# Prompt attention of a decoder step: branch A's probabilities turned by matrix products with a scaled identity

## The reference, cut to what matters

```python
s = jnp.where(valid, einsum(q, k), -inf)
p = softmax(s)                      # branch A
o_a = einsum(p, v)

p = softmax(scores)                 # branch B
a = p[:, :, 0] - lam * p[:, :, 1]
o_b = rmsnorm(einsum(a, v), subln_g) * (1 - lam_init)
```

## Time and profile before

| | us |
|---|---|
| median of 3 runs | 3218.79 |
| lowest and highest run | 3216.23 and 3221.10 |
| the profiled execution: time, and its span from first to last instruction | 3220.68, 3219.1 |
| TensorE busy in the span | 2871.2 |
| VectorE busy in the span | 1445.2 |
| ScalarE busy in the span | 587.4 |

### The profile page before, as it was taken

One profiled execution on the slowest core, in us unless ns is written; L12 is line 12 of the kernel. 1 busy time (PEld: TensorE's weight loads), 2 busy tenths in 40 slices (PEclk: granted clock), 3 DMA queues, 4 the chain that ended last, 5 costly groups with the idle time before them and its releaser, 6 DMA issues. The chain is left out here.

```text
span 3219.1 us, 69051 instructions
## 1 busy us (share of the span) xinstructions
PE 2871.2 (89%) x26593; PEld 2016.6 (63%) x26593; DVE 1445.2 (45%) x2844; ACT 587.4 (18%) x1308; POOL 678.1 (21%) x1192
## 2 busy tenths in 40 slices
PE   8998979999888669999988799999798799998698
PEld 4764534665566446666755566766566576675698
DVE  2337858995778364333343543333433632002211
ACT  2431112101666010101010110100100201001101
POOL 0131003001200001133432433333333333430000
PEclk9999989999999889999998999999899799999799
DMA  7575239422500857788997989889888796762585
GB/s 230 145 221 189 79 104 304 144 80 68 181 11 17 245 175 248 251 304 294 324 304 268 319 274 310 290 306 309 283 295 277 259 305 229 227 204 90 183 265 193
DMA packets 419890, 708.71 MB, mean 220 GB/s; under 512 B 67985, under 2 KB 230193, under 8 KB 419442
## 3 DMA queue, kind: packets, MB, share of 16 engines
q1 hardware_dynamic: 330674, 470.65, 44.8%
q0 software_dynamic: 75456, 232.86, 21.9%
q10 hardware_dynamic: 13440, 0.85, 0.3%
HBM read 660.01 MB, written 92.13 MB: 234 GB/s over the span
## 5 line engine op out<-in xcount | busy, mean ns | idle before, releaser
L1457 PE MATMUL sa_t<-tw_z,tw_w 128*128 128x304 f32 x2496 | 681.3, 429 | 15.5 <-DVE tw_z L1534 11.1
L1457 PEld LDWEIGHTS sa_t<-tw_z,tw_w 128*128 128x128 f32 x2496 | 471.9, 193 | 196.1 <-issue 44.7
L1735 POOL DMA_DIRECT2D sa_ring_v<-cache_b_kv x512 | 275.2, 537 | 1207.7 <-PE sa_o L1864 813.0
L1457 PE MATMUL sa_t<-tw_x,tw_w 128*128 128x304 f32 x1440 | 405.8, 439 | 41.6 <-DMA tw_w<-packed 35.3
L1975 DVE STREAM_TRANSPOSE sa_key_b<-sa_ring_k 128x2048 f32<-128x2048 f32 x128 | 294.8, 2306 | 260.6 <-PE sa_s L1797 192.5
L1457 PEld LDWEIGHTS sa_t<-tw_x,tw_w 128*128 128x128 f32 x1440 | 278.3, 198 | 149.1 <-issue 62.6
L414 PE MATMUL pr_acc<-pr_w,pr_u_t 128*128 128x512 f32 (+1 forms) x720 | 288.3, 549 | 3.7 <-DVE pr_row L574 3.7
L1736 POOL DMA_DIRECT2D sa_ring_va<-cache_a_kv x512 | 274.1, 535 | 54.1 <-issue 27.4
L874 PE MATMUL sel_g<-sel_u,sel_gw 128*128 128x352 f32 x768 | 227.5, 460 | 0.0
L1797 PE MATMUL sa_s<-sa_key_b,sa_q_pad 32*32 32x256 f32 x8192 | 189.2, 410 | 26.2 <-DVE sa_key_b L1975 19.5
L874 PEld LDWEIGHTS sel_g<-sel_u,sel_gw 128*128 128x128 f32 x768 | 146.1, 190 | 81.7 <-issue 0.8
(11 more groups left out here) (334 smaller groups left out, 3475.7 us busy)
## 6 DMA issues: line engine op xcount, KB each, us to landing
sa_ring_k<-cache_b_kv SPq DMA_DIRECT2D x512, 256.0 KB, 3.9
sa_ring_v<-cache_b_kv POOLq DMA_DIRECT2D x512, 256.0 KB, 6.3
tw_w<-packed SPq DMA_DIRECT2D x228, 512.0 KB, 6.6
tp_w<-packed SPq DMA_DIRECT2D x76, 512.0 KB, 4.3
sa_ring_ka<-cache_a_kv SPq DMA_DIRECT2D x512, 64.0 KB
sa_ring_va<-cache_a_kv POOLq DMA_DIRECT2D x512, 64.0 KB, 6.1
packed<-w_gate_up POOLq DMA_DIRECT2D x44, 512.0 KB, 14.3
tw_w<-packed SPq DMA_DIRECT2D x48, 256.0 KB, 7.3
```

Source lines behind the costliest of these rows:

```text
L1457: ins = pe.matmul(bank[:, 0:self.width], self.w[:, at % self.SLOTS, k - lo, :], moving[:, k, :], start=(k == 0), stop=(k == depth - 1))
L1735: pool.dma_start(ring_v[:, n % RING, :], rows_of(cache_b, page, 1)).then_inc(v_in[n // 4 % 2], 16)
```

## The change

Branch A's probabilities are divided while they are turned. VectorE's mix of an A unit makes two identities with their rows multiplied by the inverse sums (spread), and TensorE turns a block by a plain product with spread in place of a transposition with ident. The product with line 1090 goes, and out only copies. In VectorE's step out now comes before mix and is of unit s - 4 in place of s - 3; the loops of all engines have one step more, and the stores and ROOT are one step later. ScalarE's fifth and later units wait for scaled or mixed in place of o_read.

```diff
-    ROOT = 8 * LAST + 3
+    ROOT = 8 * LAST + 4
...
-        inverse_of = ph.sb("inverse_of", [P, 2, 2, DH])
+        inverse_a = ph.sb("inverse_a", [P, 2])
+        spread = ph.sb("spread", [P, 2, 2, P])
...
                 def transposes(u):
                     if kind == "a":
-                        pe.wait_ge(exped, 2 * u + 2)
+                        pe.wait_ge(scaled, u // 2 + 1)
...
-                            ins = pe.transpose(t_bank[n % 2][:, b - lo, :], src[:, b * P:(b + 1) * P], ident[:])
+                            if kind == "a":
+                                ins = pe.matmul(t_bank[n % 2][:, b - lo, :], src[:, b * P:(b + 1) * P], spread[:, u // 2 % 2, m], start=True, stop=True)
+                            else:
+                                ins = pe.transpose(t_bank[n % 2][:, b - lo, :], src[:, b * P:(b + 1) * P], ident[:])
...
                 def values(u):
-                    if kind == "a":
-                        pe.wait_ge(scaled, u // 2 + 1)
-                        pe.matmul(scale_a, inverse_of[:, u // 2 % 2]..., ident[:], start=True, stop=True, skip_group_check=True)
...
-                                ins = pe.matmul(o_a[rows], va[:, b, rows], prob_t[...], start=False, stop=(b == i),
+                                ins = pe.matmul(o_a[rows], va[:, b, rows], prob_t[...], start=(b == 0), stop=(b == i),
...
                 def exps(u, m):
                     if u >= 4 and m == 0:
-                        act.wait_ge(o_read, u - 3)
+                        act.wait_ge(*((scaled, u // 2 - 1) if UNITS[u][1] == "a" else (mixed, b_before[u - 4] + 1)))
...
                 def mix(u):
                     if kind == "a":
                         dve.wait_ge(exped, 2 * u + 2)
+                        nc.vector.reciprocal(inverse_a[:], total[:, u % 4, :])
+                        dve.drain()
                         if u >= 4:
-                            dve.wait_ge(pv_done, u - 3)
-                        nc.vector.reciprocal(inverse_of[:, u // 2 % 2], total[:, u % 4, :]...to_broadcast([P, 2, DH])).then_inc(scaled, 1)
+                            dve.wait_ge(turned, turned_by[u - 4])
+                        for m in range(2):
+                            ins = nc.vector.tensor_scalar(spread[:, u // 2 % 2, m], ident[:], inverse_a[:, m:m + 1], None, ALU.mult)
+                        ins.then_inc(scaled, 1)
...
                 def out(u):
-                        nc.vector.tensor_copy(scale[:], scale_a)
-                        dve.drain()
-                        nc.vector.tensor_tensor(o_ta[:, k % 2, r, :], o_a, scale[:], ALU.mult).then_inc(o_read, 1)
+                        nc.vector.tensor_copy(o_ta[:, k % 2, r, :], o_a).then_inc(o_read, 1)
...
-                for s in range(U + 3):
+                for s in range(U + 4):
                     if s < U:
                         mask(s)
+                    if s >= 4:
+                        out(s - 4)
                     if 1 <= s < U + 1:
                         mix(s - 1)
-                    if s >= 3:
-                        out(s - 3)
```

More of the change, by code:

```diff
@@ L1024, in prompt_attend @@
         weight = ph.sb("weight", [P, 2])
-        inverse_of = ph.sb("inverse_of", [P, 2, 2, DH])
+        inverse_a = ph.sb("inverse_a", [P, 2])
+        spread = ph.sb("spread", [P, 2, 2, P])
         squares = ph.sb("squares", [P, P])
-        scale = ph.sb("scale", [P, P])
         ms = ph.sb("ms", [P, TILES * H_B])
@@ L1035, in prompt_attend @@
         o_bank = [ph.ps(f"o{c}", [P, 512]) for c in range(2)]
-        o_a, scale_a, o_b = o_bank[0][:, 0:P], o_bank[0][:, P:2 * P], o_bank[1][:, 0:P]
+        o_a, o_b = o_bank[0][:, 0:P], o_bank[1][:, 0:P]
         packed = ph.sem("packed")
@@ L1087, in values @@
                         pe.wait_ge(o_read, u - 1)
-                    if kind == "a":
-                        pe.wait_ge(scaled, u // 2 + 1)
-                        pe.matmul(scale_a, inverse_of[:, u // 2 % 2].rearrange("p m d -> p (m d)"), ident[:], start=True, stop=True, skip_group_check=True)
                     pe.wait_ge(t_copied, turned_by[u])
@@ L1095, in values @@
                                 rows = slice(m * DH, (m + 1) * DH)
-                                ins = pe.matmul(o_a[rows], va[:, b, rows], prob_t[:, u % 2, m, b, :], start=False, stop=(b == i),
+                                ins = pe.matmul(o_a[rows], va[:, b, rows], prob_t[:, u % 2, m, b, :], start=(b == 0), stop=(b == i),
                                                 tile_position=(0, m * DH), skip_group_check=True)
@@ L1114, in _ @@
                         transposes(s - 2)
-                    if s >= 3:
+                    if 3 <= s < U + 3:
                         values(s - 3)
@@ L1154, in copy_tile @@
                     act.sem_inc(b_copied, 1)
-                for s in range(1, U + 3):
+                for s in range(1, U + 4):
                     if s - 1 < U:
@@ L1190, in store_b @@
                     sp.dma_start(a["o_t"][512:1024, i * P:(i + 1) * P].rearrange("(h e) t -> e h t", e=P), o_tb[:, j % 2]).then_inc(b_stored[j % 2], 16)
-                for s in range(U + 3):
-                    if s >= 9 and (s - 9) % 8 == 0 and (s - 9) // 8 < TILES:
-                        store_a((s - 9) // 8)
+                for s in range(U + 4):
+                    if s >= 10 and (s - 10) % 8 == 0 and (s - 10) // 8 < TILES:
+                        store_a((s - 10) // 8)
                     if 0 <= s - ROOT - 1 < LAST:
@@ L1219, in mix @@
                         dve.wait_ge(exped, 2 * u + 2)
+                        nc.vector.reciprocal(inverse_a[:], total[:, u % 4, :])
+                        dve.drain()
                         if u >= 4:
-                            dve.wait_ge(pv_done, u - 3)
-                        nc.vector.reciprocal(inverse_of[:, u // 2 % 2], total[:, u % 4, :].rearrange("p (m o) -> p m o", o=1).to_broadcast([P, 2, DH])).then_inc(scaled, 1)
+                            dve.wait_ge(turned, turned_by[u - 4])
+                        for m in range(2):
+                            ins = nc.vector.tensor_scalar(spread[:, u // 2 % 2, m], ident[:], inverse_a[:, m:m + 1], None, ALU.mult)
+                        ins.then_inc(scaled, 1)
                         return
```

## The result

| | before | after |
|---|---|---|
| median of 4 runs each, us | 3217.75 | 3250.89 |
| lowest and highest | 3216.23, 3221.10 | 3247.73, 3255.82 |
| the profiled execution: time, span | 3220.68, 3219.1 | 3247.73, 3246.1 |

The ratio is 1.0103 (95%: 1.0085 to 1.012): the change costs 33 us by the medians, 27 by the two profiled executions. The forecast was 3246, its range 3230 to 3264.

A forecast was written before the change was run, and what follows sets the result against it. No single engine was taken to bound the stage: a VectorE-TensorE chain in small-A pairs, TensorE in large ones. Periods gave +25.8 us, one clock fall brought +27.5, added to the median 3218.79: 3246, own range 3236 to 3256, with rivals 3230 to 3264.

The forecast's parts named there:

- Price of a product: A's turned blocks on TensorE: 0.235 us a product, +0.118 a block over a transposition, +34.0 us for 288 blocks.
- doubt about four times: A's turned blocks: by the skill's fourfold transposing speed a product would take 0.47 us, adding 101 us in place of 34.
- The new wait: A's products wait for VectorE's scaled identity: 1.60 us from the end of B's masks, TensorE's wait near 1.0 in A0.
- Periods: Eight tile-pair periods in the prompt's attention: sum 66.23 us against 59.77, +6.46.
- From periods to stage: Eight periods, each four times, make up the attention stage: +6.46 becomes +25.8 us.
- The clock: TensorE's granted clock in the stage: one more fall after idling, 1.7 us.
- The end of the stage: Stage ends and later stores: same instructions, costed at nothing; uncovered, one store's wait would be about 1 us.
- One to one into the span: Attention stage, closed by barriers on both sides: its gain or loss goes fully into the span, nothing else touched.
- Only large A tiles pay: Rival, 12 in 100: scaling ready in time, small pairs unchanged, four large ones grow; +12.7 us, 3231.5.
- Clock falls in A0 to A2: Rival, 13 in 100: each of these 12 pairs loses 1.5 us at half clock; +18 more, 3263.
- VectorE's relief decides: Rival, 2 in 100: products cost no more than transpositions, 0.60 us a pair saved 32 times; 3199.6.
- Fourfold: Rival, 1 in 100: a product takes four transpositions' time on TensorE; +91 us, about 3310.

The follow-up runs named there:

- e1: Kernel before, with A's blocks turned by plain products with the unscaled identity, division and line 1090 kept; 3283.64 us, ratio 1.0179.
- e3: Changed kernel with VectorE's order put back to mask, mix, out (out still of unit s - 4); 3247.41 us, ratio 1.0078 to before.
- e2: Changed kernel with A's blocks turned by plain transpositions, still waiting for the scaled identity, A's output undivided; 3250.78 us, ratio 1.0086 to before.
- f1: e1 with 48 small unread products (192 TensorE instructions) added at the stage's end; ratio 1.0072 to before, median 21.4 us above it.
- g4: e4 with 128x2 reciprocal, ScalarE's earlier wait, and output after mix in steps masking A's tiles 5 to 7; ratio 0.9999 to before.
- f3: Changed kernel with 16 small unread products (64 TensorE instructions) added at the stage's end; ratio 1.0079 to before, median 26.3 us above it.
- e4: Kernel before with only the order changed: out of unit s - 4 ahead of mix, steps and stores one later; 3220.51 us, ratio 1.0001.
- g2: e3 with 16 small unread products (64 TensorE instructions) added at the stage's end; ratio 1.0081 to before, median 22.5 us above it.
- f2: Kernel before with 16 small unread products (64 TensorE instructions) added at the stage's end; ratio 1.0126, median 41.2 us above before.
- g1: e2 with 32 small unread products (128 TensorE instructions) added at the stage's end, A's output undivided; ratio 1.0003 to before.

## Why the prediction was right, and where it was off

- **Price of a product: right.** Sixteen products go from 847.49 to 851.26, 0.236 each, for 0.235 taken. e1's stage, with products and nothing else, grew by 24.4. The second pass of each f32 product is the change's whole cost in the stage. The forecast's doubt about four times (the Trainium skill, TensorE: Matmul & The Clock Gate, section Terms) is answered by these rows: twice.
- **The new wait: right in kind, near in size.** From the end of the B masks to the products it is 1.47 for 1.60, the wait 0.84 for 1.0. Of it, at A0, B's output ahead of the scaling costs 0.70: the difference between the third and the fourth period of A0 after (7.65, when no B output exists yet, and 8.36) and between after and e3 (7.66). e2 shows that outside A0 and A1 wait, order and the loss of line 1090 together are level or a gain, up to 0.27 a pair.
- **Periods: the sum right (66.42 for 66.23), single ones off by up to 0.47.** A7 is 0.16 longer, because the lone B transposition takes 0.26 up to the next start (852.00 to 852.26) and not 0.12. A4 was taken for a chain of VectorE's (8.15) and is TensorE's, 8.05 of 8.62 busy. A2 and A3 are 0.25 and 0.34 shorter: the branch over ScalarE was drawn too long. These cancel.
- **From periods to stage: too high.** 25.8 became 22.3. The first two periods of the stage, while the pipeline fills and the clock is not yet full, took 8.01 and 8.00 us, 8.00 and 7.97 before, and the third has no B output yet (7.65 for 7.41), so the four pairs of A0 grew by 1.2 and not by 4.0. That was the pipeline's filling, which "eight periods, each four times" passes over.
- **The clock: its price right, its sign wrong.** One more fall was expected, +1.7. Instead two of before went. Busy times of before and of after around them (A7's and the last tile's stretches):

```profile
825.19:859.64 34.45, 30.76 (x254) 22.26 (x254) 23.38 (x69) 21.57 (x53) 14.91 (x18) 0.95 0.77 241
...
1010.25:1036.96 26.71, 22.91 (x176) 16.74 (x176) 21.27 (x62) 18.64 (x42) 0.00 (x0) 0.94 0.09 21
```

```profile
826.98:862.75 35.77, 33.70 (x296) 26.32 (x296) 21.68 (x75) 22.00 (x50) 14.52 (x18) 1.00 0.75 232
...
1029.47:1055.67 26.20, 23.74 (x195) 17.50 (x193) 17.80 (x60) 18.05 (x42) 0.00 (x0) 1.00 0.06 11
```

  In the first, four pairs of A7 cost 1.3 instead of 4 x 0.76 = 3.0; in the second three pairs of A4 became 0.5 shorter. The waits that had stood ahead of the falls were 1.66 and 2.24 at 1029.58. The first is 1.49 in after, and that the shorter wait saved the clock is not shown. e1 and f1 run the same instructions up to there, and the same wait of 1.67 has a fall behind it in e1 and none in f1; the eight transposes show it:

```profile
829.96 1.82 PE L1084 MATMUL att_t<-keep_ident,att_diff 128*128 128x128 f32 x8 [1.67 <-DVE att_diff L1236]
```

```profile
830.73 1.09 PE L1084 MATMUL att_t<-keep_ident,att_diff 128*128 128x128 f32 x8 [1.67 <-DVE att_diff L1238]
```

  The granted clock in the 2 us from there was 0.55 and 1.00, and the two periods around it took 20.31 and 18.74: one fall costs 1.6 us, and whether it comes behind this wait differs between two executions of the same stage. g4 had one behind 1.30, and f3, the changed kernel's own stage, had one in A1 (a period of 9.05 for 8.10). The second fall went with its wait. The wait is gone in e4, where only the order differs (that period is 8.53 for 11.66), and it is 1.63 without a fall in e1, where only the products differ (10.63). So the order alone takes that wait away, and the first fall was lost by luck.
- **The end of the stage: costed at nothing, 4.1 longer in this execution.** From A4's last scores on it takes 30.4 instead of 26.2. Of that 1.4 comes with the products alone (27.6 in e1) and was counted in the four times eight periods. The rest is the doubt of the forecast, "uncovered, one store's wait would be about 1 us": it was uncovered. All of B's tiles are turned a step later, so the last ones come close on each other, and ScalarE waits for the store of a tile two earlier; ScalarE and TensorE after:

```profile
1077.61 0.58 ACT L1151 COPY att_o_tb<-att_t 128x512 f32<-128x512 f32 x1 [2.26 <-DMA o_t<-att_o_tb]
1078.66 0.20 ACT L1175 ACTIVATE att_root<-att_ms 128x4 f32<-128x4 f32 x1 [0.46 <-issue]
```

```profile
1080.34 1.11 PE L1107 MATMUL att_t<-keep_ident,att_o_rows 128*128 128x128 f32 x4 [5.77 <-DVE att_o_rows L1267]
```

  The root behind that copy is late, so TensorE's last wait is 5.77 where it was 3.02 at 1057.51. Most of that belongs to this one execution: the same store's wait is 0.42 in f3, e3 and g2, where TensorE's last wait is 3.7 to 3.9 and the end takes 28.5 to 28.7. Wait and copy together are 1.0 there, as the forecast had feared, and 2.8 in after.
- **"One to one into the span": wrong.** The barrier separates the work, not the instruction stream. Outside the stage the medians hold some 10 us, but about 5 for the same kernel at shift 0 (f3) and for g2, and no run settles how much. The forecast had +27.5 in the stage and nothing behind it; it was 22.3 and the rest. Filling and lost clock falls took away about what the end and the rest added, so that 3246 lay so near 3251 was in part luck.
- **Rivals.** Only large A tiles pay: no, A0 grew to 8.36. Clock falls in A0 to A2: no; the pairs of A0 have 0.80 of the clock, 0.78 before, both from the start of the stage, and A1's and A2's 1.00. VectorE's relief decides: 0.58 a pair is there, and with line 1090 gone it only pays for the wait (e2's periods). Fourfold: no.

## What to carry to other kernels

An f32 product with an identity costs two passes where a transposition costs one; folding a scale into it did not pay here, where TensorE was busy in 85% of the stage before. Price a steady period, but then write out the first and last few of the pipeline by hand, stores included. And before a difference of one per cent is put down to an edit in a program of many small matmuls, shift the instructions behind it by a few dozen: here 16 idle products were worth more than the change.

## What the runs showed of the hardware that was not expected

The time of unchanged code depended on how many TensorE instructions stood before it: 41 us for 64 instructions (f2), and e1, off by the same 64, got 44 us back with 192 more (f1; 34 by the ratios), with a period that fits 256. The waits are up to 3.5 us long (g1), end 1.2 to 1.6 us behind the landing of a packet of instructions, stand at fixed instructions, and some are followed by a granted clock near 0.5, others, of the same length, by 1.00 (3.16 us, at 1893 in f2). Of f2's 18 waits above 1 us 13 stand at the 2048 32x256 products of one line (1809, which is 1807 in before), out of 21955 products in that part; why there stays open. A granted clock of 1.00 was kept over a wait of 1.49 us in the stage after (for the difference, at 833.55). Before it fell behind one of 1.66, and behind waits of 1.67 it did both (e1 and f1).
